# Gaps between the chunks of TensorE's moving operands in a two-block transformer kernel on Trainium2

## The chip, the cores and the metric

One Trainium2 chip, one core of it. The metric is the device time of one launch in microseconds. Before the change it is 3458.23 us, the median of three runs (3457.17 to 3460.68).

## The reference

Two blocks of two layers each work on one sequence of 512 tokens with 1024 features, all in fp32. What matters here is that most of the arithmetic is dense products of the sequence with weight matrices:

```
# first block, per layer
proj = h @ w_in[l]                                   # 1024 x 2610
mixed = concat(nsa_mixer, gla_mixer, pool_mixer)
h = layer_norm(ALPHA * h + mixed @ w_out[l])
ff = square(relu(h @ w_up[l])) @ w_down[l]           # 1024 x 4096 x 1024
h = layer_norm(ALPHA * h + ff)

# second block, per layer
h = h + 0.5 * rms_norm(swiglu(rms_norm(h), ffn_wi[i, 0], ffn_wo[i, 0]))   # 1024 x 5632, 2816 x 1024
h = h + rms_norm(mixer(rms_norm(h)))                 # dilated or windowed attention
h = h + 0.5 * rms_norm(swiglu(rms_norm(h), ffn_wi[i, 1], ffn_wo[i, 1]))
h = h + rms_norm((p[i] @ ple_proj[i]) * sigmoid(rms_norm(h) @ ple_gate[i]))
```

## The kernel before, in words

The activations stand transposed in SBUF: 128 features on the partitions, 512 tokens along the free axis, so 1024 features are eight chunks. A dense product is made of fp32 values that are split in two fp32r parts, a high one and a low one. Three matmuls of 128x128 weights by 128x512 activations stand for one fp32 product: high by high, high weights by low activations, low weights by high activations. `piece` (lines 869 to 874) issues the three; `abreast` (lines 908 to 928) issues the same three in another order for the first tiles of a stage, where the chunks of the input become ready one by one.

**Weights** come as a stream of units of 128x1024 fp32 from HBM by SP's queue into `raw` (line 640). ScalarE makes the high part `wh` (line 1547), VectorE the low part `wl` (line 2024). `raw`/`wl` and `wh` are rings of four buffers of 4096 bytes a partition each. A unit holds eight 128x128 weight chunks of 512 bytes a partition, so `piece` takes columns `kc % 8 * P` of a unit. A few units (at the joints of stages) go to two buffers of their own, `wl_apart` and `wh_apart`.

**Moving operands** are four tensors, each with a high and a low part of 512 tokens for each chunk, 4096 bytes a partition for both:

```
x   = at("x",   [P, DC, 2, S], F32R)      # eight chunks: the input of every dense stage
mid = at("mid", [P, FF2C, 2, S], F32R)    # 22 chunks: what lies between the two products of a feed-forward stage
px  = at("px",  [P, 2, 2, S], F32R, offset=x_at + 6 * 2 * S * 4)   # over chunks 6 and 7 of x
ao, bo                                    # outputs of the two attention mixers, over mid
```

`at` hands out byte offsets within a partition one after another, beginning at 16512, so every address follows from the listing. `h` takes 16384 bytes, `x` begins at 32896 and takes 32768, `y` follows with 16384, then the rings, and `mid` begins at 135168. Modulo 512 bytes this makes: `x` and `px` 128, the rings `wl` and `wh` 128, `mid` and `ao` 0, `bo` 192. Of the buffers apart, one pair (over `mid`) is at 0 and the other (over `y`) at 128. A chunk of 4096 bytes, a half chunk of 2048 bytes and a weight chunk of 512 bytes keep these remainders, so a moving operand has one distance to its weights, modulo 512, in all its chunks.

The order of the work on every engine is fixed at build time, by generators such as `plan_n`, `plan_a` and `plan_b` for the mixers and by plain loops for the rest. Semaphores join the engines: `split_done` tells TensorE that a unit's weights are ready, `unit_done` tells ScalarE and SP that a unit is used up, `bank_free[b]` that a PSUM bank was read.

Of the kernel before, what the change touches and what calls it, by code (L numbers as in the profile page):

```python
# [20 lines left out]
F32R = mybir.dt.float32r  # L21
# [4 lines left out]
P = 128  # L26
S = 512
D = 1024
DC = D // P
# [5 lines left out]
FF2C = 2816 // P  # L35
HD = 64
N_CMP = 31
BIG_NEG = -1.0e30
FLOOR = -1.0e20


Q0, KC, VC, KS, KW, VS, VW, GV, GQ, GQX, GK, GKX, GO, PU = 0, 3, 4, 5, 6, 7, 8, 9, 12, 13, 14, 15, 16, 19
# [346 lines left out]
def build(nc, stream, x_t, p_t, small, vecs, tab1, tab_a, tab_b, consts, out):  # L389
    n_units = stream.shape[0]  # L390
    with ExitStack() as ctx:
        place = [16512]

        def at(name, shape, dt=F32, offset=None):

            size = int(np.prod(shape[1:])) * 4
            if offset is None:
                offset = place[0]
                place[0] += (size + 31) // 32 * 32
            return nc.alloc_sbuf_tensor_at(name, shape, dt, offset=offset)  # L400

        def sem(name):
            s = ctx.enter_context(nc.semaphore(name))
            return s
# [1 line left out]

        h = at("h", [P, DC, S])
        x_at = place[0]
        x = at("x", [P, DC, 2, S], F32R)
        y_at = place[0]  # L410
        y = at("y", [P, DC, S])
        px = at("px", [P, 2, 2, S], F32R, offset=x_at + 6 * 2 * S * 4)
        raw = [at(f"raw{i}", [P, UNIT]) for i in range(4)]
        wl = [at(f"wl{i}", [P, UNIT], F32R, offset=place[0] + (i - 4) * UNIT * 4) for i in range(4)]
        wh = [at(f"wh{i}", [P, UNIT], F32R) for i in range(4)]
# [8 lines left out]
        ones = at("ones", [P, P])  # L424
        vec = at("vec", [P, V_N])
        mix_at = place[0]
        mid = at("mid", [P, FF2C, 2, S], F32R)
        assert place[0] <= 229368, place[0]


# [45 lines left out]
        assert o <= mix_at + FF2C * 2 * S * 4  # L476

        emb = at("emb", [P, DC, S], offset=mix_at)
        apart_at = [mix_at + 6 * 2 * S * 4, y_at]
        raw_apart = [at(f"raw_apart{i}", [P, UNIT], offset=o) for i, o in enumerate(apart_at)]  # L480
        wl_apart = [at(f"wl_apart{i}", [P, UNIT], F32R, offset=o) for i, o in enumerate(apart_at)]
        wh_apart = [at(f"wh_apart{i}", [P, UNIT], F32R, offset=o + UNIT * 4) for i, o in enumerate(apart_at)]
# [17 lines left out]


        raw_in = [sem(f"raw_in{i}") for i in range(4)]
        apart_in = sem("apart_in")
        hi_done = sem("hi_done")
        split_done = sem("split_done")
        unit_done = sem("unit_done")
# [1508 lines left out]
        def _(dve):  # L2015
# [15 lines left out]
            def link(ins):  # L2031
                ins.then_inc(dve_step, 1)
                c.wait(dve_step)
# [271 lines left out]
            def scores(layer, s):  # L2305
# [14 lines left out]
                if t == 0:  # L2320
# [5 lines left out]
                    link(dve.tensor_reduce(out=mxc[:, :, :], in_=four, axis=AX.X, op=ALU.max))  # L2326
                    link(dve.tensor_scalar(mxc[:, :, :], mxc[:, :, :], FLOOR, None, ALU.max))
                    top = mxc[:, :, :].rearrange("p g (t o) -> p g t o", o=1).broadcast_to([P, 2, QT, 32])
# [591 lines left out]
```

## Time and profile before

| | |
|---|---|
| median of three runs | 3458.23 us (3457.17 to 3460.68) |
| profiled execution, span from first to last instruction | 3455.3 us |
| TensorE matmul (PE) busy | 3347.0 us, 97%, 16570 instructions |
| TensorE weight load (PEld) busy | 2636.1 us, 76% |
| VectorE (DVE) busy | 1834.0 us, 53% |
| ScalarE (ACT) busy | 1241.7 us, 36% |
| GpSimd (POOL) busy | 342.6 us, 10% |
| mean granted clock of TensorE | 0.989 |
| read from HBM | 296.14 MB, 86 GB/s over the span |

The profile states the profiled execution by its span alone, 3455.3 us; its whole time is not among the three runs. PE is the engine that multiplies, PEld the loading of weights into it, which overlaps the multiplication. A matmul's own duration is longer than the distance from its start to the next one's start, since matmuls are pipelined; a busy time is the union of them. "L872" is line 872 of the kernel. In `bank<-x,wh` the tile `bank` is written, `x` moves through the array and `wh` stands in it.

### The profile page before, as it was taken

To read this page: it belongs to the slowest core of one execution; us is meant where nothing else is said; L and a number is where in the kernel's file an instruction comes from. 1 tells how busy PE (TensorE), PEld (TensorE's weight loads), DVE (VectorE), ACT (ScalarE), POOL (GpSimd) and SP (SyncE) were. 2 spreads that over 40 slices of the span, in tenths; PEclk is the share of its full clock that TensorE was granted. 3 is DMA by queue.
4 is the path that set the end of the run, shared out by engine and by line. 5 is a ranking of instruction groups with operands and counts; after the bars stand their busy time and mean duration, and the time that the engine had idled before them with its cause. 6 is when DMAs were issued, how large, how long until landed. Compare 5 with 4: busy or idle time off the path is not lost.

```text
span 3455.3 us, 42531 instructions
## 1 busy us (share of the span) xinstructions
PE 3347.0 (97%) x16570; PEld 2636.1 (76%) x16570; DVE 1834.0 (53%) x2932; ACT 1241.7 (36%) x1878; POOL 342.6 (10%) x244
## 2 busy tenths in 40 slices
PE   9999999999899999999999999999999989999997
PEld 6667888776688887888777778887788866688886
DVE  5766334567752446443566664435644357654436
ACT  3354223424442324332333343224433235533324
POOL 0310000212100020000233100000000012000001
PEclk9999999999999999999999999999999999999999
DMA  4102222311122222223322222232222321132232
GB/s 161 62 31 74 93 96 98 125 65 49 50 86 92 97 92 85 97 97 100 109 74 68 66 78 95 97 104 92 85 97 97 100 92 44 56 104 97 97 102 76
DMA packets 81431, 300.35 MB, mean 87 GB/s; under 512 B 9040, under 2 KB 9040, under 8 KB 80640
## 3 DMA queue, kind: packets, MB, share of 16 engines
q1 hardware_dynamic: 78624, 284.20, 24.7%
q0 software_dynamic: 1568, 11.98, 0.9%
q8 instruction: 103, 1.69, 0.2%
q10 hardware_dynamic: 1088, 2.10, 0.2%
q14 instruction: 48, 0.39, 0.0%
HBM read 296.14 MB, written 2.10 MB: 86 GB/s over the span
## 4 chain that ended last, share of the span: by engine, by line
PE 90%; DVE 5%; ACT 3%; issue 1%; POOL 1%; DMA 1%; ACTq 0%; DVEq 0%; POOLq 0%
PE bank L872 26%; PE bank L874 25%; PE bank L873 25%; PE bank L916 2%; PE bank L917 2%; PE bank L923 2%; DVE wl L2024 1%; PE bank L1409 1%; ACT sc L1708 1%; PE bank L1173 1%; PE bank L1421 1%; PE bank L1188 1%; PE bank L1154 1%; PE bank L1464 1%; PE bank L1112 1%
## 5 line engine op out<-in xcount | busy, mean ns | idle before, releaser
L872 PE MATMUL bank<-x,wh 128*128 128x512 f32 x2632 | 1054.5, 401 | 12.2 <-DVE h L2468 5.7
L874 PE MATMUL bank<-x,wl 128*128 128x512 f32 x2632 | 1028.3, 391 | 0.0
L873 PE MATMUL bank<-x,wh 128*128 128x512 f32 x2632 | 1026.8, 390 | 0.0
L1547 ACT ACTIVATE wh<-raw 128x1024 fp32r<-128x1024 f32 x528 | 558.1, 1058 | 1196.3 <-PE bank L874 1108.0
L2024 DVE TENSOR_TENSOR wl<-raw,wh 128x1024 fp32r<-128x1024 f32 x528 | 677.2, 1283 | 581.3 <-ACT wh L1547 580.1
L872 PEld LDWEIGHTS bank<-x,wh 128*128 128x128 f32 x2632 | 494.9, 188 | 133.2 <-issue 25.9
L874 PEld LDWEIGHTS bank<-x,wl 128*128 128x128 f32 x2632 | 495.1, 188 | 105.8
L873 PEld LDWEIGHTS bank<-x,wh 128*128 128x128 f32 x2632 | 495.9, 188 | 98.5 <-issue 3.4
L872 PE MATMUL bank<-mid,wh 128*128 128x512 f32 x1216 | 482.1, 396 | 0.0
L874 PE MATMUL bank<-mid,wl 128*128 128x512 f32 x1216 | 480.3, 395 | 0.0
L873 PE MATMUL bank<-mid,wh 128*128 128x512 f32 x1216 | 480.2, 395 | 0.0
L872 PEld LDWEIGHTS bank<-mid,wh 128*128 128x128 f32 x1216 | 228.3, 188 | 56.4 <-issue 1.0
L873 PEld LDWEIGHTS bank<-mid,wh 128*128 128x128 f32 x1216 | 228.3, 188 | 56.1 <-issue 1.0
L874 PEld LDWEIGHTS bank<-mid,wl 128*128 128x128 f32 x1216 | 228.3, 188 | 55.5
L2163 DVE TENSOR_TENSOR prod<-bank,rs_in 128x512 f32<-128x512 f32 x88 | 60.7, 690 | 232.3 <-PE bank L874 232.3
L2040 DVE TENSOR_TENSOR mid<-prod,mid 128x512 f32 (+1 forms) x152 | 104.8, 689 | 88.3 <-ACT mid L1848 85.5
L675 POOL TENSOR_TENSOR acc<-sq,sq 128x512 f32<-128x512 f32 x8 | 11.2, 1397 | 1305.5 <-ACT sq L1653 1305.5
L916 PE MATMUL bank<-x,wh 128*128 128x512 f32 x200 | 85.5, 428 | 46.6 <-ACT x L1604 23.8
L2480 DVE TENSOR_TENSOR prod<-tmp,bank 128x512 f32<-128x512 f32 x64 | 43.9, 686 | 142.7 <-ACT tmp L1798 142.7
L1848 ACT ACTIVATE mid<-prod 128x512 f32 (+1 forms) x88 | 55.6, 632 | 174.6 <-DVE prod L2528 174.6
L1798 ACT ACTIVATE tmp<-bank 128x512 f32<-128x512 f32 x64 | 38.1, 596 | 178.5 <-PE bank L874 178.5
L2163 DVE TENSOR_TENSOR tmp<-bank,rs_in 128x512 f32<-128x512 f32 x88 | 60.8, 691 | 59.8 <-PE bank L874 58.6
(340 smaller groups left out, 3297.4 us busy)
## 6 DMA issues: line engine op xcount, KB each, us to landing
raw<-stream SPq DMA_DIRECT2D x528, 512.0 KB, 3.3
raw_apart<-stream SPq DMA_DIRECT2D x10, 512.0 KB, 3.6
sm<-small POOLq DMA_DIRECT2D x2, 2144.0 KB, 9.6
tb<-tab POOLq DMA_DIRECT2D x2, 1728.0 KB, 13.8
h<-x_t ACTq DMA_DIRECT2D x4, 512.0 KB, 7.0
out_t<-h SPq DMA_DIRECT2D x8, 256.0 KB, 2.1
tba<-tab_a POOLq DMA_DIRECT2D x1, 1152.0 KB, 7.8
pf<-p_t POOLq DMA_DIRECT2D x2, 512.0 KB, 3.7
```

Source lines behind the costliest of these rows:

```text
L872: pe.matmul(dst, hi, src[:, kc, 0, :], start=start, stop=False)
L873: pe.matmul(dst, hi, src[:, kc, 1, :], start=False, stop=False)
L874: return pe.matmul(dst, lo, src[:, kc, 0, :], start=False, stop=stop)
L916: pe.matmul(dst, hi, x[:, kc, 0, :], start=kc == 0, stop=False)
L917: pe.matmul(dst, lo, x[:, kc, 0, :], start=False, stop=False)
L923: mm = pe.matmul(dst, hi, x[:, kc, 1, :], start=False, stop=kc == 7)
L1547: act.activation(high_of(n)[:, :], raw_of(n)[:, :], ACT.Copy).then_inc(hi_done, 1)
L1848: act.activation(mid[:, i * 2 + k, 0, :], prod[k][:, :], ACT.Copy).then_inc(mid_hi, 1)
L2024: dve.tensor_tensor(low_of(n)[:, :], raw_of(n)[:, :], high_of(n)[:, :].bitcast(F32), ALU.subtract).then_inc(split_done, 1)
L2040: dve.tensor_tensor(dst, src, hi.bitcast(F32), ALU.subtract).then_inc(done, 1)
L2163: free(dve.tensor_tensor(dst, bank[c.peek()][:, :], rs_in[:, :], ALU.mult))
L2480: free(dve.tensor_tensor(prod[k % 2][:, :], tmp[k % 2][:, :], b[:, :], ALU.mult))
```

## The change

`x`, `px` and `mid` get a gap behind each chunk: 4 fp32 (16 bytes) in `x` and `px`, 8 fp32 (32 bytes) in `mid`. The chunk pitch becomes 4112 bytes in `x` and 4128 in `mid`; the high and the low part of one chunk stay 2048 bytes apart. The place of `y` and of all that follows is rounded up, 512 bytes above where it was, so that the remainders modulo 512 of `y`, of the rings and of the start of `mid` stay what they were. One of the two buffer pairs apart moves with `mid`'s pitch, to remainder 192. `ao` and `bo` are laid out as before. With the rings at 128, chunk k of `x` is then 16*k bytes from its weights modulo 512 (0 to 112), and chunk k of `mid` 384 + 32*k modulo 512, which goes once round all sixteen multiples of 32 and on to the 22nd chunk.

No instruction is added, removed or moved on any engine; only addresses differ.

```diff
+X_GAP, MID_GAP = 4, 8
...
+        def staggered(name, chunks, gap, offset=None):
+
+            t = at(name, [P, chunks, 2 * S + gap], F32R, offset)
+            return t[:, :, 0:2 * S].rearrange("p k (e s) -> p k e s", e=2)
+
...
         x_at = place[0]
-        x = at("x", [P, DC, 2, S], F32R)
+        x = staggered("x", DC, X_GAP)
+        place[0] += (x_at - place[0]) % 512
         y_at = place[0]
         y = at("y", [P, DC, S])
-        px = at("px", [P, 2, 2, S], F32R, offset=x_at + 6 * 2 * S * 4)
+        px = staggered("px", 2, X_GAP, x_at + 6 * (2 * S + X_GAP) * 4)
...
-        mid = at("mid", [P, FF2C, 2, S], F32R)
+        mid = staggered("mid", FF2C, MID_GAP)
...
-        apart_at = [mix_at + 6 * 2 * S * 4, y_at]
+        apart_at = [mix_at + 6 * (2 * S + MID_GAP) * 4, y_at]
```

## Rows read from the trace of the kernel before

**Rows 1.** The page: span, and busy time of each engine.
```profile
span 3455.3 us, 42531 instructions
PE 3347.0 (97%) x16570; PEld 2636.1 (76%) x16570; DVE 1834.0 (53%) x2932; ACT 1241.7 (36%) x1878; POOL 342.6 (10%) x244
```
**Rows 2.** The page: the chain that ended last, by engine.
```profile
PE 90%; DVE 5%; ACT 3%; issue 1%; POOL 1%; DMA 1%; ACTq 0%; DVEq 0%; POOLq 0%
```
**Rows 3.** Groups: busy us, mean ns, idle before and its releaser.
```profile
L872 PE MATMUL bank<-x,wh 128*128 128x512 f32 x2632 | 1054.5, 401 | 12.2 <-DVE h L2468 5.7 <-DVE wl L2024 5.1 <-DVE x L2040 1.3
L874 PE MATMUL bank<-x,wl 128*128 128x512 f32 x2632 | 1028.3, 391 | 0.0
L873 PE MATMUL bank<-x,wh 128*128 128x512 f32 x2632 | 1026.8, 390 | 0.0
L872 PE MATMUL bank<-mid,wh 128*128 128x512 f32 x1216 | 482.1, 396 | 0.0
L874 PE MATMUL bank<-mid,wl 128*128 128x512 f32 x1216 | 480.3, 395 | 0.0
L916 PE MATMUL bank<-x,wh 128*128 128x512 f32 x200 | 85.5, 428 | 46.6 <-ACT x L1604 23.8 <-ACT x L1587 12.2 <-DVE wl L2024 10.7
```
**Rows 4.** Windows, matmuls that read x: us, PE busy (count), clock, DMA.
```profile
480.00:560.00 80.00, 80.00 (x355) 1.00 0.30 99
1400.00:1500.00 100.00, 100.00 (x443) 1.00 0.30 100
3100.00:3200.00 100.00, 100.00 (x443) 1.00 0.29 95
```
**Rows 5.** Windows, matmuls that read mid.
```profile
390.00:470.00 80.00, 80.00 (x345) 1.00 0.28 92
2260.00:2360.00 100.00, 100.00 (x430) 1.00 0.31 101
2700.00:2800.00 100.00, 100.00 (x431) 1.00 0.32 106
```
**Rows 6.** Window, matmuls that read bo.
```profile
2985.00:3003.00 18.00, 18.00 (x81) 1.00 0.35 118
```
**Rows 7.** Timeline of PE, px with the weights apart: start, us; 24 matmuls, then the next.
```profile
2375.52 0.40 PE L872 MATMUL bank<-px,wh_apart 128*128 128x512 f32 x1
...
2380.88 0.40 PE L874 MATMUL bank<-px,wl_apart 128*128 128x512 f32 x1
2381.11 0.39 PE L916 MATMUL bank<-x,wh 128*128 128x512 f32 x1
```
**Rows 8.** Timeline of PE, px with the ring's weights, just behind an interruption.
```profile
2371.62 0.40 PE L873 MATMUL bank<-px,wh 128*128 128x512 f32 x1
2371.85 0.40 PE L874 MATMUL bank<-px,wl 128*128 128x512 f32 x1
2372.09 0.40 PE L872 MATMUL bank<-px,wh 128*128 128x512 f32 x1
...
2373.70 0.39 PE L873 MATMUL bank<-px,wh 128*128 128x512 f32 x1
2373.93 0.39 PE L874 MATMUL bank<-px,wl 128*128 128x512 f32 x1
```
**Rows 9.** Timeline, all engines, in a stretch of x: a weight load beside a matmul.
```profile
480.09 0.39 PE L873 MATMUL bank<-x,wh 128*128 128x512 f32 x1
480.09 0.19 PEld L874 LDWEIGHTS bank<-x,wl 128*128 128x128 f32 x1
480.31 0.39 PE L874 MATMUL bank<-x,wl 128*128 128x512 f32 x1
```
**Rows 10.** Groups within 480:560, x in its steady pace.
```profile
L873 PE MATMUL bank<-x,wh 128*128 128x512 f32 x118 | 45.9, 389 | 0.0
```
**Rows 11.** Groups within 2985:3003, bo: three matmuls of a chunk.
```profile
L872 PE MATMUL bank<-bo,wh 128*128 128x512 f32 x27 | 10.6, 394 | 0.0
L873 PE MATMUL bank<-bo,wh 128*128 128x512 f32 x27 | 10.5, 388 | 0.0
```
**Rows 12.** Groups: the two halves of the weight split, and what they wait for.
```profile
L2024 DVE TENSOR_TENSOR wl<-raw,wh 128x1024 fp32r<-128x1024 f32 x528 | 677.2, 1283 | 581.3 <-ACT wh L1547 580.1
L1547 ACT ACTIVATE wh<-raw 128x1024 fp32r<-128x1024 f32 x528 | 558.1, 1058 | 1196.3 <-PE bank L874 1108.0 <-PE bank L923 44.6 <-DMA raw<-stream 41.8
```

## The prediction

> **What bounds the kernel now.** I read the page's busy times first: matmuls fill 97% of the span, the other engines 53% and less [rows 1]. The chain of waits agrees: 90% of it is PE [rows 2]. The groups say which matmuls: 7,896 by line 872 to 874 that read `x`, 3,648 that read `mid`, and some 800 in the order of `abreast` (L916, L917, L923) [rows 3]. No idle time stands before most of them. The split of the weights is covered: ScalarE's half sits idle for 1196.3 us, mostly waiting for PE to use up a unit, and VectorE's half waits for ScalarE's [rows 12]. So what counts is the pace of the large matmuls, from the start of one to the start of the next, and the change can act on nothing else, since it leaves every instruction and every wait in its place.
>
> The windows give that pace. A window of 100 us holds 443 matmuls on `x` (one or two of them cut by its edges), which is 226.7 ns each, and the same in a stage near the end of the kernel [rows 4]. It holds 430 to 431 on `mid`, 233.3 ns each [rows 5]. Both at the full granted clock of 2.4 GHz (1.00), with the same weights ring, the same kind of instruction and similar DMA traffic (95 to 106 GB/s). Each matmul has the load of the next weights beginning beside it [rows 9]. What differs is the address of the moving operand: `x` stands 0 bytes from its weights modulo 512, `mid` 384. Two other distances occur. `bo` is at 64: 81 matmuls in 18 us less the cut ones, about 229 ns [rows 6]. `px` against the weights apart is at 128: 24 matmuls from 2375.52 to 2381.11, so 5.59 / 24 = 233 ns [rows 7]. This stretch holds settling at its beginning, and its last repeats look like the first, so I take 232.5.
>
> A distance has no fixed price by itself, though. `px` against the ring is at distance 0, like `x`. Yet behind an interruption ten matmuls, from 2371.62 to 2373.93, take 2.31 us, 231 ns each [rows 8], and only then fall to `x`'s 226.7. With `bo` the three matmuls of one chunk last 394 and 388 ns, in turn [rows 11]. So a matmul's loss depends on the distance and on the moment at which it starts relative to something that its predecessors set, and a constant distance lets the sequence settle into a repeating pattern. Distance 0 settles at the best of the four.
>
> By the Trainium skill, page "TensorE: Matmul & The Clock Gate", section "Back-to-back issue gap", a 512-column matmul at 2.4 GHz follows its predecessor after 512/2.4 + 2.5 = 216 ns. The trace shows 226.7 at best in a steady stretch, so 10.9 ns on `x` and 17.5 on `mid` are a loss by that rule.
>
> **The change part by part.** It has two address terms and nothing that is added or removed.
>
> *Term 1, `x` and `px`.* The eight chunks go from distance 0 to 0, 16, ... 112. The nearest rows are distance 0 (226.7), 64 (229) and 128 (232.5). Straight lines between them, over the eight chunks, give a mean of 229.0: a gain over `x`'s present pace is not in reach of these rows, and this is the lower end. The upper end is the unsettled pace of 231 [rows 8], with a margin to 232, since every third matmul now changes its distance and the sequence has three matmuls to settle where it took ten. I take 230.5, nearer to the unsettled row, since a chunk gives no time to settle. Which matmuls lose this? Those that run settled now. In the steady stretch a matmul lasts 389 ns [rows 10], unsettled 390 to 400; the mean over all is 390 and 391 for L873 and L874 [rows 3]. With unsettled ones at about 394, 20 to 30% are unsettled, so some 6,200 of 7,896 are settled. 6,200 x 3.8 ns = **+23.6 us** (+14 to +33). The other 1,700 and the 800 of `abreast` are mixed already: -0.5 ns each, **-1 us**.
>
> *Term 2, `mid`.* Its chunks go from 384 alone to all sixteen multiples of 32. The mean of the four distances with a row is (226.7 + 229 + 232.5 + 233.3) / 4 = 230.4, and the unsettled row again says 231. I take 231.0: 3,648 x -2.3 ns = **-8.4 us** (from -12.8 at 229.8 to -2.9 at 232.5).
>
> *Everything else* is at nothing. `ao`, `bo` and `y` keep their remainders. ScalarE and VectorE write the same 128x512 halves at other addresses; were they slower, ScalarE's 1196.3 us of idle time before the split would hide it [rows 12]. By the Trainium skill, page "SBUF — State Buffer", section "SBUF: two separate sides", lines of SBUF are 16 bytes; all new starts are multiples of 16, so a matmul would touch as many lines as before. No run here shows it. Were a coarser unit the one that counts, that is the last rival below.
>
> The sum: 23.6 - 1 - 8.4 = +14 us. Against the profiled execution's span of 3455.3 us that is 3469.5; the median of the runs stands 2.9 us above that span, for what lies around it, so 3472. The forecast's own range is from +1.5 (lowest x term, highest gain on `mid`) to +31: 3460 to 3489. A measurement of this kernel can tell about 0.2%, 7 us, from no change.
>
> **The rivals.**
>
> *Faster: the collisions thin out.* What is lost over the best matmuls is a meeting of two reads, the moving operand's and the weights'. Distances that differ might make it rarer than any constant one does, and `mid` has the most to give. For it: the pace does depend on the distance, and 0 may not be the best of the 32 distances in steps of 16; no row shows any distance that is not a multiple of 64, and `x` gets six of those among eight. The 388 ns of `bo`'s second matmul [rows 11] is below `x`'s settled 389, so better single matmuls exist. Against: of the four distances seen, 0 is the best for a long stretch and its two neighbours upward are worse. It decides as soon as `x` loses less than 3,648 x 2.3 / 6,200 = 1.4 ns, that is a mean under 228.1. Price: `x` unchanged and `mid` at 229 is -16 us, 3442. If both come to 225, `x` gives 6,200 x 1.7 + 1,700 x 6 = -21 and `mid` 3,648 x 8.3 = -30: 3407. Chance 0.29.
>
> By the page's 216 ns, were all loss gone, the time would fall by some 150 us; nothing in the trace reaches that pace.
>
> *No change.* The two terms cancel (x +1.4 ns on average), or the difference between `x` and `mid` has another cause than the distance, the place of `mid` in SBUF for one. Against the second: `x` with weights apart and `px` at distance 128 also differ from `x`. That is within 7 us of 3458. Chance 0.13. The same TensorE page, section "Step-by-step: what each phase is for", speaks for it: the moving operand and the weight load have independent read ports, and the one takes no bandwidth from the other. By that rule term 1 and term 2 would both be 0. The trace speaks against it: 226.7 and 233.3 ns with identical instructions.
>
> *Slower by much: starts off a 64-byte boundary cost.* All four tensors start at multiples of 64 now. After the change six of eight chunks of `x` and eleven of 22 of `mid` do not. If such a read took one more step, of a length like the difference between `x` and `mid`, 6.6 ns, it would cost 7,896 x 0.75 x 6.6 + 3,648 x 0.5 x 6.6 = +51 us in place of the terms or on top of them: 3509 to 3523. It decides from the point where a start off the boundary costs more than the forecast's 3.8 ns. Nothing in the trace shows or excludes it. Chance 0.06.
>
> **How the numbers follow.** The forecast has 0.52, the faster rival 0.29, no change 0.13, the costly starts 0.06. The forecast's lower edge runs into no change (+1.5 us), so I count 0.03 of its chance there. So faster 0.29, same 0.13 + 0.03 = 0.16, slower 0.49 + 0.06 = 0.55. The predicted time is the likeliest case's, 3472. The range takes in the forecast's own range and no change, and reaches down to 3425 to hold over half of the faster rival; upward it ends at 3492. Left out are some 0.13 below and 0.06 above. Since cases of both signs hold much of the chance, the forecast's own range, 3460 to 3489, stands beside it.
>
> **What would show it right or wrong.** The counts in windows of 100 us: on `x` 434 to 436 instead of 443, on `mid` 434 to 435 instead of 430. Settled matmuls of 389 ns in long runs should be gone from `x`, and its L873 and L874 groups should have means near 393 ns. If the `x` windows hold 443 or more, term 1 is wrong; if a window holds over 450, the faster rival is right and the range with it in danger. If chunk 0 of `x` differs from chunk 7 by the same amount in every tile, the distance alone prices a matmul; if they read alike, the sequence does. If ScalarE, VectorE or DMA groups change their means by over 1%, something outside this argument has moved.

## The result and the profile after

The changed kernel takes 3485.51 us, the median of four runs (3481.92 to 3489.97), against 3458.18 us for the kernel before, four runs beside them. The ratio is 1.0079 with a 95% interval of 1.0066 to 1.0093: 27 us slower. The forecast was 3472 us with a range of 3425 to 3492, and slower as the likeliest sign. The direction and the range held; the size was short by half.

The page of the changed kernel, against [rows 1] and [rows 2]: span and busy times, then the chain by engine.

```profile
span 3486.8 us, 42531 instructions
PE 3379.4 (97%) x16570; PEld 2637.9 (76%) x16570; DVE 1834.8 (53%) x2932; ACT 1241.7 (36%) x1878; POOL 342.7 (10%) x244
...
PE 90%; DVE 5%; ACT 3%; issue 1%; POOL 1%; DMA 0%; DVEq 0%; ACTq 0%; POOLq 0%
```

The span grew by 31.5 us and PE's busy time by 32.4 us. VectorE, ScalarE and GpSimd moved by under 1 us, and the chain has the same shares. So all of it is in matmuls that follow each other more slowly. The groups, whose lines are seven higher than in [rows 3] and [rows 12] (columns: busy us, mean ns, idle before and its releaser):

```profile
L879 PE MATMUL bank<-x,wh 128*128 128x512 f32 x2632 | 1067.2, 405 | 12.5 <-DVE h L2475 5.4
L881 PE MATMUL bank<-x,wl 128*128 128x512 f32 x2632 | 1038.0, 394 | 0.0
L880 PE MATMUL bank<-x,wh 128*128 128x512 f32 x2632 | 1035.9, 394 | 0.0
L1554 ACT ACTIVATE wh<-raw 128x1024 fp32r<-128x1024 f32 x528 | 558.3, 1058 | 1218.3 <-PE bank L881 1125.6
L2031 DVE TENSOR_TENSOR wl<-raw,wh 128x1024 fp32r<-128x1024 f32 x528 | 677.0, 1283 | 585.5 <-ACT wh L1554 584.3
...
L879 PE MATMUL bank<-mid,wh 128*128 128x512 f32 x1216 | 482.6, 397 | 0.0
L881 PE MATMUL bank<-mid,wl 128*128 128x512 f32 x1216 | 480.4, 395 | 0.0
L880 PE MATMUL bank<-mid,wh 128*128 128x512 f32 x1216 | 477.7, 393 | 0.0
```

On `x` the two clean groups went from 391 and 390 ns to 394 and 394. ScalarE's split of the weights kept its 1058 ns and VectorE's its 1283; ScalarE waits longer for PE (1218.3 us idle where it was 1196.3), and VectorE for ScalarE. Last the windows, against [rows 4] and [rows 5] (us, PE busy and count, granted clock, DMA share, GB/s), first `x`:

```profile
490.00:560.00 70.00, 70.00 (x303) 1.00 0.27 90
1400.00:1500.00 100.00, 100.00 (x433) 1.00 0.28 94
```

and `mid`:

```profile
2270.00:2370.00 100.00, 100.00 (x432) 1.00 0.32 105
```

A window counts every matmul that overlaps it, and each lasts 0.39 us, so the pace is (window + 0.39) / count. This document uses that for all kernels, the one before included. A count is a whole number, so a pace read in this way can be off by 0.5 ns in a window of 100 us and by 0.9 ns in one of 60 us; where a smaller difference matters, below, it is read from the starts of the matmuls themselves. On `x` it is 100.39 / 433 = 231.8 ns where it was 100.39 / 443 = 226.6. On `mid` it is 232.4 where it was 100.39 / 430 = 233.5. With the prediction's counts this gives 6,200 x 5.2 = +32 us and 3,648 x -1.1 = -4 us, together +28; measured are +27.

### The profile page after: what moved, and what is told of

Read it like the earlier page. It is cut to its first block, busy times and chain, and to the rows that moved or that the text cites. A ratio compares the mean times of both kernels' runs of the same rounds, so it can differ in the third digit from the quotient of the medians.

```text
span 3486.8 us, 42531 instructions
## 1 busy us (share of the span) xinstructions
PE 3379.4 (97%) x16570; PEld 2637.9 (76%) x16570; DVE 1834.8 (53%) x2932; ACT 1241.7 (36%) x1878; POOL 342.7 (10%) x244
## 4 chain that ended last, share of the span: by engine, by line
PE 90%; DVE 5%; ACT 3%; issue 1%; POOL 1%; DMA 0%; DVEq 0%; ACTq 0%; POOLq 0%
PE bank L879 26%; PE bank L881 25%; PE bank L880 25%; PE bank L923 2%; PE bank L924 2%; PE bank L930 2%; DVE wl L2031 1%; PE bank L1416 1%; ACT sc L1715 1%; PE bank L1180 1%; PE bank L1428 1%; PE bank L1195 1%; PE bank L1161 1%; PE bank L1471 1%; PE bank L1119 1%
## 5 line engine op out<-in xcount | busy, mean ns | idle before, releaser
L879 PE MATMUL bank<-x,wh 128*128 128x512 f32 x2632 | 1067.2, 405 | 12.5 <-DVE h L2475 5.4
L880 PE MATMUL bank<-x,wh 128*128 128x512 f32 x2632 | 1035.9, 394 | 0.0
L1554 ACT ACTIVATE wh<-raw 128x1024 fp32r<-128x1024 f32 x528 | 558.3, 1058 | 1218.3 <-PE bank L881 1125.6
L2031 DVE TENSOR_TENSOR wl<-raw,wh 128x1024 fp32r<-128x1024 f32 x528 | 677.0, 1283 | 585.5 <-ACT wh L1554 584.3
L923 PE MATMUL bank<-x,wh 128*128 128x512 f32 x200 | 87.3, 437 | 46.6 <-ACT x L1611 23.8
```

Of the source, the lines that this page charges most:

```text
L879: pe.matmul(dst, hi, src[:, kc, 0, :], start=start, stop=False)
L880: pe.matmul(dst, hi, src[:, kc, 1, :], start=False, stop=False)
L923: pe.matmul(dst, hi, x[:, kc, 0, :], start=kc == 0, stop=False)
L1554: act.activation(high_of(n)[:, :], raw_of(n)[:, :], ACT.Copy).then_inc(hi_done, 1)
L2031: dve.tensor_tensor(low_of(n)[:, :], raw_of(n)[:, :], high_of(n)[:, :].bitcast(F32), ALU.subtract).then_inc(split_done, 1)
```

## The experiments

Two theories were set against each other, and a third against both:

- **Settling**: the distance sets a pace only once the sequence has settled; changing the distance from chunk to chunk keeps it from settling, and that is what costs.
- **Price by distance**: each distance has its pace, and gaps average over good and bad ones.
- **Boundary**: a start off a 64-byte boundary costs by itself.

All twelve kernels are made from the kernel before with the same four numbers, two of them with one more edit that is told in its place (`lead` is in fp32 units, so a shift of 16 bytes is possible; the rings keep remainder 128):

```diff
+X_SHIFT, X_GAP, MID_SHIFT, MID_GAP = 0, 0, 0, 0
...
+        def staggered(name, chunks, gap, offset=None, lead=0):
+            n = chunks * (2 * S + gap)
+            t = at(name, [P, lead + n], F32R, offset)
+            t = t[:, lead:lead + n].rearrange("p (k w) -> p k w", k=chunks)
+            return t[:, :, 0:2 * S].rearrange("p k (e s) -> p k e s", e=2)
...
-        x = at("x", [P, DC, 2, S], F32R)
+        x = staggered("x", DC, X_GAP, None, X_SHIFT // 4)
+        place[0] += (128 - place[0]) % 512
...
+        place[0] += MID_SHIFT
         mix_at = place[0]
-        mid = at("mid", [P, FF2C, 2, S], F32R)
+        mid = staggered("mid", FF2C, MID_GAP)
```

`px` follows `x`, and the buffers apart follow `mid`'s place and pitch. The results in one place; "before" is the kernel before beside the same runs, and a ratio stands where a kernel was timed more than once:

| kernel | x: distance | mid: distance | us | before | ratio (95%) |
|---|---|---|---|---|---|
| x_part | 0 to 112 by 16 | 384 | 3487.04 | 3457.32 | 1.0082 (1.0065 to 1.0099) |
| mid_part | 0 | 384 + 32 k | 3455.29 | 3457.32 | 0.9994 (0.9984 to 1.0004) |
| mid_zero | 0 | 0 | 3432.59 | 3457.32 | 0.9925 (0.9909 to 0.9942) |
| x16_mid64 | 16 | 64 | 3472.30 | 3457.32 | 1.0039 (1.0025 to 1.0053) |
| x_gap64 | 0 to 448 by 64 | 384 | 3483.05 | 3459.11 | 1.0074 (1.0058 to 1.0091) |
| all_off32 | 0 | 0 | 3433.46 | 3459.11 | 0.9931 (0.9914 to 0.9947) |
| x32_mid256 | 32 | 256 | 3477.88 | 3459.11 | one run |
| x496_mid448 | -16 | -64 | 3516.81 | 3459.11 | one run |
| x_gap256 | 0 and 256 by turns | 0 | 3430.68 | 3456.88 | 0.9921 (0.9904 to 0.9938) |
| x48_mid96 | 48 | 96 | 3496.28 | 3456.88 | one run |
| x112_mid160 | 112 | 160 | 3483.34 | 3456.88 | one run |
| all_zero | 0 | 0, bo too | 3431.74 | 3456.97 | 0.9926 (0.9912 to 0.9939) |

### The two parts alone

`X_GAP = 4`, all else 0:

> Only x and px get their gaps, mid stays at distance 384. If the pace of the matmuls is all there is (settling theory, and price-by-distance alike): x holds 432 to 433 matmuls in 100 us, mid 430, and the time is 3.5 to 5 us above the whole change, 3489 to 3493 us. If the places of x and mid acted together in some other way, the parts do not add up to the +27 us of the whole.

`MID_GAP = 8`, all else 0:

> Only mid gets its gaps, x stays at distance 0. Both theories: x holds 443 in 100 us, mid 432, time 3.5 to 5 us below before, about 3454 us.

Measured: +29.7 us with `x` alone and -2.0 us with `mid` alone, the latter inside what can be told from no change. The sum, +27.7, is near the whole's +27.3; the intervals of x_part and of the whole are some 5 us wide to either side, so that they agree to 0.4 us is luck. The `x` window of x_part and that of mid_part:

```profile
1400.00:1500.00 100.00, 100.00 (x433) 1.00 0.26 94
```
```profile
1400.00:1500.00 100.00, 100.00 (x443) 1.00 0.27 94
```

So `x`'s gaps are the loss. The parts don't act quite apart, though. The window on `mid` in x_part:

```profile
2270.00:2370.00 100.00, 100.00 (x432) 1.00 0.30 105
```

430 were expected and stand in the kernel before, since `mid` has no gaps here and keeps its distance of 384. By the starts of the matmuls its pace is 232.4 ns on the average of all stages, where it was 233.3, and x_gap64 has 232.4 as well. In both kernels the rings and `mid` lie 512 bytes higher than before, at the same distance; which of this moves the pace stays open. It is worth 3,648 x -0.9 = -3 us, so `x`'s own loss is about 33 us where x_part shows +29.7, and `mid`'s gaps, at 232.3 in the changed kernel, bring next to nothing once `x` has its own.

### mid brought to x's distance

`MID_SHIFT = 128`, no gaps:

> No gaps; all that starts at mid's place is moved up by 128 bytes, so mid is at distance 0 from its weights in all chunks, like x. Distance theory (settling or price): mid runs at x's pace, 226.7 ns, 441 matmuls in 100 us, 3648 x 6.6 ns = 24 us faster than before, 3434 us. Rival, that mid is slower because of where it lies in SBUF or what feeds it: mid keeps 430 in 100 us and the time stays at 3458 us.

Measured 3432.59 us, 24.7 us under the kernel before; 24 were expected. The windows on `mid`:

```profile
400.00:470.00 70.00, 70.00 (x311) 1.00 0.29 98
2270.00:2350.00 80.00, 80.00 (x355) 1.00 0.32 112
```

70.39 / 311 = 226.3 and 80.39 / 355 = 226.5 ns: `mid` has `x`'s pace. One added number moved it there, so the difference between `x` and `mid` in the kernel before was the distance and nothing else of `mid`.

### Constant distances, and the boundary

`X_SHIFT = 16, MID_SHIFT = 192`:

> No gaps; x and px at a constant distance of 16 bytes, mid at a constant 64. Mid: at bo's pace, 229 ns or 436 to 437 in 100 us, by the distance theories. For x: the theory that a start off a 64-byte boundary costs by itself expects 231 ns or more (433 or fewer in 100 us), all chunks being off the boundary. The settling theory expects a short repeating pattern at a pace of its own, under the 232.0 ns that x has in the changed kernel. Time if x keeps 226.7: 3442 us; if x is at 232: 3486 us.

The window on `x`, then one on `mid`:

```profile
1400.00:1500.00 100.00, 100.00 (x434) 1.00 0.27 94
```
```profile
400.00:460.00 60.00, 60.00 (x263) 1.00 0.28 96
```

`mid` at 64 has 60.39 / 263 = 229.6, near `bo`'s pace. `x` at a constant 16 has 231.3 ns. That is hardly under the 231.8 of the changed kernel although the distance never changes, a blow to the settling theory in its plain form, and just what the boundary theory expected. The next run moves `h` and all that follows up by 32 bytes (the first place from 16512 to 16544, the rounding from 128 to 160) on top of mid_zero:

> The kernel with mid at distance 0, and every tensor of SBUF moved up by 32 bytes: moving operands and weights all start 32 bytes off a 64-byte boundary, at distance 0 throughout. Distance theory: 226.7 ns on x and mid, 3432 to 3433 us as before the move. Boundary theory: about 5 ns more on each of some 12,000 matmuls, 3485 us or more.

```profile
1400.00:1500.00 100.00, 100.00 (x443) 1.00 0.28 94
```

443 again, and 3433.46 us: -25.7 us against its own kernel before, where mid_zero had -24.7. Every operand is now off the 64-byte boundary and nothing is lost, so the boundary theory falls. It is the distance between the two operands that counts and not the remainder of the moving one: `x` begins at 160 modulo 512 here and in x32_mid256 below, and the same window holds 443 with the rings at 160 and 430 with the rings at 128. (Whether a start 16 bytes off would behave otherwise than 32 at distance 0 was not tried.)

`X_GAP = 16`, 64 bytes, keeps the boundary and changes the distance:

> x and px with gaps of 64 bytes (distances 0, 64, ... 448, every start on a 64-byte boundary), mid as before. The boundary theory (a start off 64 bytes costs about 5 ns, which the 231.7 ns of x at a constant 16 would also bear out) expects x near the aligned distances' own paces, 226.7 to 231, and the x windows at 434 to 440 in 100 us: 3458 to 3480 us. The theory that changing the distance from chunk to chunk keeps the sequence unsettled expects the same 232 ns as with gaps of 16 bytes, 432 to 433 in 100 us, 3487 us.

```profile
1400.00:1500.00 100.00, 100.00 (x433) 1.00 0.28 94
```

The same 433 as with gaps of 16 bytes, +23.9 us. This again speaks against the boundary theory, and it is the number that the theory of an unsettled sequence named; what the sequence does is read further down.

### More of the map, and its period

`X_SHIFT = 32, MID_SHIFT = 384`; then `X_SHIFT = 496, MID_SHIFT = 64`:

> Constant distances of 32 bytes (x) and 256 (mid), one look at the paces. Distance theory: each settles in a short pattern of its own, above 226.7; by the rows so far x between 229 and 232 ns, mid at 232 or 233. Boundary theory: x at 231 to 232 again, mid free of it.

> Constant distances of -16 bytes (x) and -64 (mid), one look. If being near 0 is what helps, whichever side, x is under its 231.7 ns at +16; if 0 alone is good, x is at 230 to 234. Mid: between 226.7 (0) and 233.3 (-128), some 229 to 233.

x32_mid256, `x` and `mid`:

```profile
1400.00:1500.00 100.00, 100.00 (x430) 1.00 0.28 94
...
2270.00:2370.00 100.00, 100.00 (x443) 1.00 0.31 106
```

`mid` at 256 has 443, where 232 or 233 ns were expected: a clear miss, and the most useful one. 256 acts like 0. On the other side of 0 there is no shelter: at -16 `x` has 424, 236.8 ns, the slowest of all and above the expected 230 to 234. `mid` at -64 has 259 in 60 us, 233.2.

```profile
1400.00:1500.00 100.00, 100.00 (x424) 1.00 0.29 94
```

The period was tested with `X_GAP = 64` (256 bytes) and `MID_SHIFT = 128`:

> x and px with gaps of 256 bytes, mid without gaps at distance 0. mid at distance 256 ran at 226.7 ns, so if what counts is the distance modulo 256 and not 512, x at distances 0 and 256 by turns stays at 226.7 ns, 443 in 100 us, and the time is that of mid at distance 0, 3433 us. If a gap costs as such, or 512 is the period, or changing the distance at all unsettles the sequence: x at 230 to 232 ns, 3460 to 3475 us.

```profile
1400.00:1500.00 100.00, 100.00 (x443) 1.00 0.29 98
3100.00:3200.00 100.00, 100.00 (x443) 1.00 0.28 94
```

Gaps that turn `x` between 0 and 256 cost nothing: 3430.68 us, -26.2. So neither the gap as such nor a change of the distance modulo 512 matters. x_gap64 bears it out for other distances: its chunks 0 to 3 and 4 to 7 are 256 bytes apart, and by their starts both fours have the paces 230.0, 232.7, 232.3 and 231.7 ns. The distance counts modulo 256 bytes, and the changed kernel's distances were chosen modulo 512.

Two more kernels, `X_SHIFT = 48, MID_SHIFT = 224` and `X_SHIFT = 112, MID_SHIFT = 288`:

> Constant distances of 48 bytes (x) and 96 (mid), one look, to fill the map. No distance so far beats 226.7 ns; between 16 (231.7), 32 (233.7) and 64 (228.9) I expect 230 to 233 on x, and 229 to 234 on mid. A pace under 226 would show a version that beats distance 0.

> Constant distances of 112 bytes (x) and 160 (mid), one look. Around 128 (233) I expect 230 to 235 on both. If the mean over all constant distances is near the 232 ns of the kernels with gaps, gaps just average the distances; if it is clearly higher or lower, the change from chunk to chunk matters by itself.

x48_mid96 in two windows on `x`:

```profile
490.00:560.00 70.00, 70.00 (x306) 1.00 0.28 91
1400.00:1500.00 100.00, 100.00 (x430) 1.00 0.28 92
```

70.39 / 306 = 230.0 ns in one stage and 233.5 in the other: the same kernel, the same distance, the same clock, two paces. The groups of the two windows show it as well, 392 ns on all three lines in the first, 396 to 395 in the second:

```profile
L881 PE MATMUL bank<-x,wh 128*128 128x512 f32 x102 | 40.0, 392 | 0.0
L882 PE MATMUL bank<-x,wh 128*128 128x512 f32 x102 | 40.0, 392 | 0.0
L883 PE MATMUL bank<-x,wl 128*128 128x512 f32 x102 | 40.0, 392 | 0.0
...
L883 PE MATMUL bank<-x,wl 128*128 128x512 f32 x144 | 57.0, 396 | 0.0
L882 PE MATMUL bank<-x,wh 128*128 128x512 f32 x143 | 56.6, 396 | 0.0
L881 PE MATMUL bank<-x,wh 128*128 128x512 f32 x143 | 56.6, 395 | 0.0
```

And x112_mid160 shows, on `x` from 1400 to 1500, a pattern that repeats with the three matmuls of a chunk:

```profile
L882 PE MATMUL bank<-x,wh 128*128 128x512 f32 x145 | 57.7, 398 | 0.0
L881 PE MATMUL bank<-x,wh 128*128 128x512 f32 x145 | 56.8, 392 | 0.0
L883 PE MATMUL bank<-x,wl 128*128 128x512 f32 x145 | 56.2, 388 | 0.0
```

All three have the same distance and last 398, 392 and 388 ns. They read different parts (high or low) of the operands, so this alone doesn't show that a matmul remembers anything. The next two windows of x112_mid160 do more. They lie in the same stage of the first block's two layers, with the same lines at the same distance and the same clock:

```profile
320.00:379.00 59.00, 59.00 (x257) 1.00 0.30 100
976.00:1035.00 59.00, 59.00 (x262) 1.00 0.30 102
```

59.39 / 257 = 231.1 ns in one and 59.39 / 262 = 226.7 in the other, the pace of distance 0, held for all of the stage's 287 matmuls. By the starts of the matmuls -16 has two paces as well, 236.7 in most stages and 233.3 in this one, in both layers. So price by distance alone falls: a distance allows one or more settled patterns, and which of them a stage falls into depends on something else. That it is what the matmuls before left behind fits [rows 8], where the pace comes down over ten matmuls, but no run shows it.

The map of constant distances modulo 256, in ns from start to start over a long stretch, read from the starts themselves: 0: 226.7; 16: 231.7; 32: 233.3; 48: 230.0 or 233.3; 64: 228.9; 96 (on `mid`): 233.3; 112: 231.1, in some stages 226.7; 128 (384): 233.3 in the kernel before, 232.4 in x_part; 160 (on `mid`): 234.3; 192 (448): 233.3; 240 (496): 236.7, in some stages 233.3. Five of the sixteen steps of 16 bytes were not tried (80, 144, 176, 208, 224), so "none is faster than 0" holds for the eleven that were.

Now the question of x112_mid160's expectation. For `x` the seven distances tried of its eight, each with the pace of most of its matmuls, have the mean (226.7 + 231.7 + 233.3 + 233.3 + 228.9 + 233.3 + 231.1) / 7 = 231.2, against 231.9 with gaps. For x_gap64 it is (226.7 + 228.9 + 233.3 + 233.3) / 4 = 230.6 against 231.7. For `mid` the seven multiples of 32 tried of eight give 231.9 against 232.3. So averaging over distances explains 4.5 of `x`'s 5.2 ns and 3.9 of x_gap64's 5.0, and 0.7 and 1.1 ns are left. This is an estimate, with one distance missing.

What is left is not a sequence that never settles. In the changed kernel a tile of `x` is 24 matmuls, three for each of eight chunks. The first matmul of three tiles in a row:

```profile
1403.67 0.40 PE L879 MATMUL bank<-x,wh 128*128 128x512 f32 x1
...
1409.24 0.40 PE L879 MATMUL bank<-x,wh 128*128 128x512 f32 x1
...
1414.81 0.40 PE L879 MATMUL bank<-x,wh 128*128 128x512 f32 x1
```

A tile takes 5.57 us each time, and each of its 24 steps from start to start is the same in tile after tile, to 1 ns, in all eight long stages of `x`. The sequence is settled, in a pattern 24 matmuls long. Counted back from the last matmul of a stage, its chunks have the paces 232.7, 232.0, 235.0, 232.7, 229.0, 231.0, 234.3 and 228.7 ns. Chunk 0, at distance 0, costs 232.7 where it costs 226.7 among neighbours at distance 0: these 6 ns on one chunk of eight are about what averaging doesn't explain. The six other chunks with a distance that was tried lie within 2.4 ns of its pace in the sum above.

### A version that beats both

mid_zero with `bo` 64 bytes higher, so that it too is at 0 modulo 256:

```diff
+        o += 64
         bo = at("bo", [P, DC, 2, S], F32R, offset=o); o += DC * 2 * S * 4
```

> mid at distance 0 as before, and bo moved up by 64 bytes to distance 0 modulo 256 as well (it stood at 233.3 ns in the kernel with mid at 0). 173 matmuls x 6.6 ns = 1.1 us less than the 3432.6 us of mid_zero: about 3431.5 us, ratio 0.992 to 0.993 to before. The bo window should show 226.7 ns, 80 to 81 in 18 us instead of 78.

3431.74 us, ratio 0.9926 (0.9912 to 0.9939): 25 us under the kernel before, 54 under the changed one. The windows on `bo`, 2965 to 2983, of mid_zero and of this one:

```profile
2965.00:2983.00 18.00, 18.00 (x78) 1.00 0.34 118
```
```profile
2965.00:2983.00 18.00, 18.00 (x81) 1.00 0.36 118
```

`bo` gains its three matmuls in 18 us: 81, as many as it has in the kernel before at distance 64 [rows 6], since at 228.9 ns against 226.7 a window of 18 us can't tell the two. The 1 us that this is worth can't be told from mid_zero by the times; all_zero, mid_zero, all_off32 and x_gap256 are one result.

## Why the prediction was right, and where its size failed

- **What bounds the kernel**: right. The whole difference is PE's busy time (+32.4 us of a span +31.5); the copies that write the gapped tensors kept their means.
- **The pace goes with the distance between moving operand and weights**: right, and shown by mid_zero, where one shift of 128 bytes gave `mid` `x`'s pace, and by all_off32, where moving both operands cost nothing.
- **Term 1, x, +23.6 us**: x_part measured +29.7, and `x`'s own part of it is about 33. Its step that failed is the straight line between the rows of distance 0, 64 and 128. It gave a mean of 229.0 ns for the eight distances; the seven tried have 231.2, because 16, 32 and 48 are no way between 226.7 and 228.9 but lie at 231.7, 233.3 and 230.0 to 233.3. The other end, 232, was nearly the result, but its reason was wrong: I said that three matmuls for each distance give no time to settle. The sequence settles into a pattern of 24, and its pace is only by chance near that of the unsettled row. The choice of 230.5 lay between a line that failed and a reason that failed.
- **Term 2, mid, -8.4 us**: mid_part measured -2.0, inside the interval of no change; by the pace it is 3,648 x -1.0 = -4 us. The four distances with a row held the two best tried (0 and 64) among four; the seven multiples of 32 tried average 231.9, not 230.4.
- **The sum and its range**: the term of -1 us stands in the sum and not in the edges. With it the forecast's own range is about 0 to +29 instead of +1.5 to +31, that is 3458 to 3487; the measured 3485.5 lies near its upper edge either way. The range of 3425 to 3492 that was given held because it was wide.
- **Everything else at nothing**: right for the copies and the other engines. Not foreseen was that `mid` changes its pace at an unchanged distance, 0.9 ns in x_part.
- **The faster rival** asked for a distance better than 0. None of the eleven tried is. Its argument that better single matmuls exist was true and of no use: x112_mid160 has lines of 388 ns under the settled 389, between others of 392 and 398. That what is lost is a meeting of two reads, as the rival has it, no run shows.
- **No change** had three grounds. That the two terms cancel is refuted by their sizes, and that `mid` is slower by its place by mid_zero. The third was independent read ports of the moving operand and the weight load (the Trainium skill, page "TensorE: Matmul & The Clock Gate", section "Step-by-step: what each phase is for": loading the next weights "doesn't steal SBUF read bandwidth from the running matmul"). The runs differ with what the prediction took from it, that the distance can't matter: with identical instructions and a granted clock of 1.00 the pace goes from 226.7 to 236.7 ns by the distance of the two addresses alone. The measurement decides; whether the ports are where it happens no run tells.
- **The costly starts** off a 64-byte boundary: refuted by all_off32 and x_gap64. Taken alone, x16_mid64 looked like its proof.
- **Of the signs I named**, the `x` window was to hold 434 to 436 and held 433; `mid` 434 to 435 and held 432; the clean groups near 393 ns had 394 and 394. All are short in the same direction as the terms. Chunk 0 was to differ from chunk 7 by the same amount in every tile if the distance alone prices a matmul, and to read alike if the sequence does. It differs, 232.7 against 228.7 ns in every tile, but the other way round than at constant distances (226.7 at 0, 231.1 at 112 in most stages), so both have a part.

## What to carry to other kernels

Where one tensor streams through TensorE while weights from another are loaded, compare the start-to-start pace of identical matmuls on different tensors before looking for anything else; if it differs, compute the operands' addresses modulo a few powers of two. Bring the slow tensor to the fast one's remainder, which costs a few bytes, rather than spreading the addresses: spreading trades the best distance for the mean of all. Interpolating an effect of addresses between a few measured distances is not safe. One run can try two distances when two tensors carry one each, and its pace should be read in several stages, since a distance can have more than one.

## What the runs showed of the hardware that was not expected

- The distance of the moving operand's start to the weights' start acts modulo 256 bytes, not 512: 256 has the pace of 0 (443 in 100 us), gaps of 256 bytes change nothing, and in x_gap64 the chunks' paces repeat after 256 bytes.
- The direction matters: 16 bytes above costs 5.0 ns a matmul (231.7 against 226.7), 16 bytes below 10.0 ns in most stages (236.7).
- At distance 0, moving both operands by 32 bytes changes nothing (443 in 100 us in all_off32). At 384 moving both by 512 bytes, in x_part, went with 232.4 ns instead of 233.3.
- Identical matmuls at a constant distance fall into settled patterns, and a distance can have several: 230.0 and 233.3 ns at 48, 231.1 and 226.7 at 112, 236.7 and 233.3 at -16, in different stages of one run. When the distance changes from chunk to chunk they settle too, into a pattern of one tile, 24 matmuls in the changed kernel. What carries the state from one matmul to the next, and what physically collides, stays open: no run here tells the mechanism.
- The paces 226.7, 230.0, 233.3 and 236.7 are 3.3 ns apart, which at the granted 2.4 GHz is 8 cycles. No run says why.
- The Trainium skill's formula for the gap of two matmuls (page "TensorE: Matmul & The Clock Gate", section "Back-to-back issue gap") gives 216 ns for 512 columns. The section calls this the gap of an isolated matmul and gives 131 ns as measured for a long stream of weight loads and matmuls. No stretch here comes near either: the best settled pace is 226.7, at every place tried, so over the formula's 216 some 10 ns of each large matmul are still unexplained.
